# Two-block transformer on one core: GpSimd's side work tied to VectorE's search rounds, and three VectorE edits beside it

## The chip, the cores and the metric

One core of one Trainium2 chip runs the whole program. The metric is the device time of one execution in microseconds; lower is better.

## The reference, cut to what matters

Two blocks of two layers each work on 512 tokens of 1024 features in float32 (the first also on 256 context tokens). The change lies in the second block:

```python
def hybrid_layer(x, ...):
    h = rms_norm_2(x, norm1_g)
    proj = h @ w_in
    (qa, ka, va, qi, ki, wi, qb, kb, vb, rb, gl, uc) = split_cols(proj)
    ...
    o_a = dsa_attention(qa, ka, va, qi, ki, wi)   # each query keeps its 128 best keys
    log_a = log_sigmoid(gl @ w_gate_up + b_gate) / 16
    o_b = gla_chunked(qb, kb, vb, log_a)          # decays between positions: exp of differences of cumsum(log_a)
    o_c = multiscale_pool(uc, w_pool, pool_scale) # trailing means over 2, 4, 8, 16 tokens, minus the token
    x = x + concat(o_a, o_b, o_c) @ w_out
    x = x + conv_glu_ffn(rms_norm_2(x, norm2_g), ...)
```

In `dsa_attention` the scores `sum_h wi * relu(qi . ki)` are masked causally, the 128 largest of each query are kept, and the rest get minus infinity ahead of the softmax. The second block begins with the first block's final norm, so its residual x has to be multiplied once by the reciprocal root of the mean square of each token (`rs_x`).

## The kernel before, in words

Tokens run along the free dimension, features along the 128 partitions. Every product with a weight is made of three matmuls, since float32 weights and activations are each held as a high and a low part (L651 to L653, and L914 to L916 where tokens go to the partitions). Weights come as slabs of 128x1024 through two raw slots; ScalarE rounds a slab to its high part (L1421), VectorE subtracts to get the low part (L2009), and only then may TensorE use it. There are two slots for split slabs: a slab's high part is made when the slab two before it has been used, its low part has to be there one slab later.

In the input stage of each layer of the second block (`in2`) VectorE is taken up by `best_keys`: for each of three query tiles (t = 1, 2, 3, with 256, 384 and 512 keys) it adds four heads of scores (L2698, L2700), masks the diagonal square (L2705, L2706), then runs 16 search rounds of "eight largest" (L2710) and "replace them" (L2711), and turns what was replaced into the mask `far` by three operations (L2714 to L2716). Meanwhile GpSimd makes the low parts of 15 slabs (`POOL_SLABS`, L2860), which I number S0 (weights of qb) to S14 (ka 0); S2 to S8 are rb 0, rb 1, va 0 to 3 and vb 0, S9 is vb 1, S10 to S13 are qa 0 to 3. Between them it does side work in a fixed order: in layer 0 it scales the eight chunks of x (`scale_x`), in both layers the gate rows, uc, four windows of the pooling (`window`), two subtractions (L2906), and the scaling of qb, kb and rb. The slab after S14 (ka 1) is VectorE's again.

Behind the search VectorE rotates the eight tiles of qa and ka (`rope`, L2247 to L2249), one for each slab. `gate_beside` puts other work behind each rotation: `gate_sums` (cumulated gates) and the first of five `distances` behind rotation 0, distances 1 and 2 behind rotation 1, 3 behind 2, 4 behind 3. ScalarE takes the exponentials of a distance in `decays`, one rotation later than the distance was queued, and VectorE multiplies them into `qd` and `kd` in `decayed`, behind rotations 2 to 6. Each engine runs its own queue in order; semaphores tie them. The products of the second attention (L1266) wait for all ten of `decayed`'s results.

Of the kernel before, what the change touches and what calls it, by code (L numbers as in the profile page):

```python
# [19 lines left out]
DC = D // P  # L20
CTX, SEQ = 256, 512
TOK = CTX + SEQ
# [35 lines left out]
NEG = -1e30  # L58
# [252 lines left out]
def build(nc, wstream, ada_w, c_in, params, x_in, rope_tab, pos_in, cnt_in, ada_first, c_cols, out):  # L311
# [3 lines left out]
    with ctx:  # L315
# [233 lines left out]
        x_scaled = sem("x_scaled")  # L549
# [839 lines left out]
        def _(act):  # L1389
# [431 lines left out]
            def in2(l):  # L1821
# [65 lines left out]
                projections(IN2_ROPED, INDEX_ROTS, beside=lambda j: decays(j - INDEX_ROTS - 1))  # L1887
# [102 lines left out]
        def _(dve):  # L1990
# [642 lines left out]
            def in2(l):  # L2633
                dsts = {"qa": qa, "ka": ka, "qi": qi}

                def results(events, j, beside=None):
                    for kind, name, g in events:
                        if kind == "idx":
                            continue
                        res.add()  # L2640
                        if kind == "gemm":
                            split_low()
                        elif kind == "rot":
                            dve.wait_ge(acc_taken, res.now())
                            dst = ki[:, :] if name == "ki" else dsts[name[0]][:, name[1], :]
                            rope(dst, rot2[j % 2][:, :], cos2[:, :], sin2[:, :]).then_inc(rot_done, 1)
                            if beside is not None:
                                beside(j)
                            j += 1

                def gate_beside(j):

                    n = j - INDEX_ROTS
                    if n == 0:
                        gate_sums(l)
                    for lev in ((0,), (1, 2), (3,), (4,))[n] if n < 4 else ():
                        distances(lev)
                    if n == 2:
                        dve.wait_ge(qk_scaled, 2 * (l + 1))
                    if 0 <= n - 2 < len(HALVES):  # L2660
                        decayed(n - 2)

                reciprocal_roots([(DC, [(0, SEQ)], D)])
                results(IN2_INDEX[:1], 0)
                if l == 0:
                    second_roots()
                results(IN2_INDEX[1:2], 0)
                copied.add()
                dve.wait_ge(rs_ready, copied.now())
                dve.wait_ge(trig_ready, 2 * (l + 1))  # L2670
                nc.vector.tensor_tensor(cos2[:, :], cos_t[:, :], rs_in[:, :], ALU.mult).then_inc(tab_made, 1)
                nc.vector.tensor_tensor(sin2[:, :], sin_t[:, :], rs_in[:, :], ALU.mult).then_inc(tab_made, 1)
                dve.wait_ge(tab_made, 2 * (l + 1))
                results(IN2_INDEX[2:], 0)
                dve.wait_ge(acc_taken, res.now())
                tables.add(16)
                pooled[l] = (res.n + 1, tables.n, copied.n, his.n)
                best_keys()
                results(IN2_PLAIN, INDEX_ROTS)
                for slabs in (4, 2):  # L2680
                    split_low(slabs)
                    res.add(QT)
                results(IN2_ROPED, INDEX_ROTS, gate_beside)
                rots.add(IN2_ROTS)

            def best_keys():
# [3 lines left out]
                for t in range(1, QT):  # L2690
# [15 lines left out]
                    v(nc.vector.tensor_tensor(score[:, diag], score[:, diag], above, ALU.add))  # L2706
# [6 lines left out]
                    b = far[:, t, 0:nk]  # L2713
                    v(nc.vector.tensor_scalar(b, work[:, 0:nk], TAKEN, NEG, ALU.is_equal, ALU.mult))  # L2714
                    v(nc.vector.tensor_scalar(b, b, -NEG, None, ALU.add))
                    v(nc.vector.tensor_tensor(far[:, t, diag], far[:, t, diag], above, ALU.subtract))  # L2716

            def gate_sums(l):

                z = tmp[2][:, :]  # L2720
                if l == 0:
                    dve.wait_ge(x_scaled, DC)
# [127 lines left out]
        def _(pool):  # L2850
# [12 lines left out]
            def scale_x(k):  # L2863
                xk = x[:, k, CTX:TOK]
                nc.gpsimd.tensor_tensor(xk, xk, rs_x[:, :], ALU.mult).then_inc(x_scaled, 1)

# [6 lines left out]

            for l in range(LAYERS):
                slabs = iter(POOL_SLABS[l])
                result, table, copied, lows = pooled[l]
                if l == 0:
                    pool.wait_ge(rs_ready, copied)
                    pool.wait_ge(hl_ready, lows)
                    for k in range(DC - 2):  # L2880
                        scale_x(k)
                pool.wait_ge(split_done, POOL_SLABS[l].start)
                split_low(next(slabs))
                if l == 0:
                    for k in range(DC - 2, DC):
                        scale_x(k)
# [3 lines left out]
                split_low(next(slabs))  # L2890
                pool.wait_ge(rope_in, table)
# [6 lines left out]
                split_low(next(slabs))  # L2898
# [3 lines left out]
                for g, width in enumerate(POOL_WINDOWS):  # L2902
                    window(g, width)
                    split_low(next(slabs))
                for c in range(2):
# [3 lines left out]
                ins.then_inc(pool_ready, 1)  # L2909
                for n, t in enumerate((qb, kb)):  # L2910
                    split_low(next(slabs))
# [248 lines left out]
```

## Time and profile before

| | |
|---|---|
| median of 3 runs | 3659.4 us (3658.09 to 3662.3) |
| the profiled execution: own time, span | 3657.96 us, 3656.1 us |
| TensorE matmul busy | 3469.6 us, 95% |
| VectorE busy | 2121.7 us, 58% |
| ScalarE busy | 1321.5 us, 36% |
| GpSimd busy | 135.6 us, 4% |
| granted TensorE clock, mean | 0.966 |
| chain of waits, share of the span | PE 83%, DVE 11%, ACT 3% |
| input stage and what follows it, layer 0 and layer 1 | from about 2300 us and from about 2970 us |

PE is TensorE, DVE VectorE, ACT ScalarE, POOL GpSimd. TensorE is busy nearly all the time, so only what lets it wait, or lowers its clock, can move the total; GpSimd's 135.6 us lie within the two input stages alone.

### The profile page before, as it was taken

The page shows a single profiled execution, that of the slowest core. Times are in us where ns is not written, and L with a number is a line of the kernel's source. Part 1 is how long each engine was busy: PE and PEld are TensorE (multiplying, and loading weights), DVE is VectorE, ACT ScalarE, POOL GpSimd, SP SyncE. Part 2 cuts the span into 40 slices and gives each one's busy share as a digit, 9 for nine tenths or more (in the row PEclk, how much of TensorE's full clock was granted, in tenths as well). Part 3 has the DMA queues.
Part 4 walks back from the last instruction along what each step waited for, and adds up shares of the span by engine and source line. Part 5 has one row for each costly group of instructions (what it writes and reads, how often), then busy time and mean ns, then how long its engine had stood idle before and what let it go on. Part 6 is the DMA issues. An engine that isn't in the chain of part 4 may idle for free.

```text
span 3656.1 us, 45965 instructions
## 1 busy us (share of the span) xinstructions
PE 3469.6 (95%) x18168; PEld 2778.6 (76%) x18168; DVE 2121.7 (58%) x3299; ACT 1321.5 (36%) x2084; POOL 135.6 (4%) x78
## 2 busy tenths in 40 slices
PE   6999999989999989999999999987999998899998
PEld 4766778878888877677777888765888877578887
DVE  4854663355575585446447664794666449646643
ACT  3344343333213223444433333334322233532222
POOL 0000000000000000000000000530000015000000
PEclk8999999999999999999999999997999999889999
DMA  5410202112351332101222333220233332013332
GB/s 232 147 41 12 87 30 86 59 52 63 109 203 63 115 116 64 30 25 45 63 87 83 95 96 103 86 76 1 92 92 93 106 98 70 30 54 96 98 96 94
DMA packets 79221, 300.56 MB, mean 82 GB/s; under 512 B 8784, under 2 KB 8912, under 8 KB 77904
## 3 DMA queue, kind: packets, MB, share of 16 engines
q1 hardware_dynamic: 77760, 291.47, 24.9%
q10 hardware_dynamic: 1296, 6.82, 0.5%
q8 instruction: 112, 1.84, 0.2%
q14 instruction: 53, 0.43, 0.0%
HBM read 296.16 MB, written 2.10 MB: 82 GB/s over the span
## 4 chain that ended last, share of the span: by engine, by line
PE 83%; DVE 11%; ACT 3%; issue 2%; DMA 1%; SPq 0%; DVEq 0%; ACTq 0%
PE ps L651 23%; PE ps L652 22%; PE ps L653 22%; PE ps L969 2%; DVE work L2711 2%; DVE top L2710 2%; PE ps L1011 1%; PE ps L1016 1%; PE ps L1039 1%; PE ps L1025 1%; PE ps L1046 1%; DVE ps L2187 1%; DVE ada_o L2187 1%; PE ps L706 1%; DVE score L2700 1%
## 5 line engine op out<-in xcount | busy, mean ns | idle before, releaser
L2009 DVE TENSOR_TENSOR split<-raw,split 128x1024 fp32r<-128x1024 f32 x412 | 504.7, 1225 | 821.8 <-ACT split L1421 820.9
L1421 ACT ACTIVATE split<-raw 128x1024 fp32r<-128x1024 f32 x442 | 466.4, 1055 | 758.3 <-PE ps L653 670.1
L651 PE MATMUL ps<-h,split 128*128 128x512 f32 x1328 | 533.4, 402 | 13.2 <-DVE split L2009 9.6
L652 PE MATMUL ps<-h,split 128*128 128x512 f32 x1328 | 526.1, 396 | 0.0
L653 PE MATMUL ps<-h,split 128*128 128x512 f32 x1328 | 525.7, 396 | 0.0
L651 PE MATMUL ps<-h_hl,split 128*128 128x512 f32 (+1 forms) x776 | 296.4, 382 | 19.5 <-DVE h_hl L2081 14.0
L651 PEld LDWEIGHTS ps<-h,split 128*128 128x128 f32 x1328 | 251.3, 189 | 80.2 <-DVE split L2009 11.7
L652 PEld LDWEIGHTS ps<-h,split 128*128 128x128 f32 x1328 | 251.3, 189 | 60.7 <-issue 2.9
L653 PEld LDWEIGHTS ps<-h,split 128*128 128x128 f32 x1328 | 251.2, 189 | 59.4
L653 PE MATMUL ps<-h_hl,split 128*128 128x512 f32 (+1 forms) x776 | 278.8, 359 | 0.0
L652 PE MATMUL ps<-h_hl,split 128*128 128x512 f32 (+1 forms) x776 | 278.6, 359 | 0.0
L651 PE MATMUL ps<-h2w,split 128*128 128x256 f32 (+1 forms) x704 | 239.9, 341 | 5.6 <-DVE h2w L2081 3.7
L652 PE MATMUL ps<-h2w,split 128*128 128x256 f32 (+1 forms) x704 | 239.7, 340 | 0.0
L653 PE MATMUL ps<-h2w,split 128*128 128x256 f32 (+1 forms) x704 | 239.3, 340 | 0.0
L653 PE MATMUL ps<-g_hl,split 128*128 128x512 f32 x528 | 208.4, 395 | 0.0
L652 PE MATMUL ps<-g_hl,split 128*128 128x512 f32 x528 | 208.4, 395 | 0.0
L651 PE MATMUL ps<-g_hl,split 128*128 128x512 f32 x528 | 208.4, 395 | 0.0
L651 PEld LDWEIGHTS ps<-h_hl,split 128*128 128x128 f32 x776 | 151.9, 196 | 56.9 <-issue 24.6
L2328 DVE TENSOR_REDUCE stat<-ps 128x1 f32<-128x768 f32 (+1 forms) x160 | 128.5, 845 | 86.5 <-PE ps L1016 81.4
L653 PEld LDWEIGHTS ps<-h_hl,split 128*128 128x128 f32 x776 | 151.4, 195 | 21.9
L652 PEld LDWEIGHTS ps<-h_hl,split 128*128 128x128 f32 x776 | 152.3, 196 | 18.2 <-issue 1.4
L1601 ACT ACTIVATE prob<-ps,stat 128x768 f32<-128x768 f32 (+1 forms) x160 | 128.9, 813 | 102.6 <-DVE stat L2328 102.6
(410 smaller groups left out, 6297.6 us busy)
## 6 DMA issues: line engine op xcount, KB each, us to landing
raw<-wstream SPq DMA_DIRECT2D x442, 512.0 KB, 3.5
ada_t<-ada_w SPq DMA_DIRECT2D x80, 512.0 KB, 4.6
first_w<-ada_first SPq DMA_DIRECT2D x4, 2048.0 KB, 24.8
x<-x_in SPq DMA_DIRECT2D x1, 3072.0 KB, 12.7
x<-x_in ACTq DMA_DIRECT2D x1, 3072.0 KB, 11.0
ada_c<-c_in SPq DMA_DIRECT2D x2, 1024.0 KB, 4.7
out<-x SPq DMA_DIRECT2D x8, 256.0 KB, 2.2
par<-params SPq DMA_DIRECT2D x1, 1345.0 KB, 5.8
```

Of the source, the lines that this page charges most:

```text
L651: nc.tensor.matmul(o, wh, a[0], start=first, stop=False)
L652: nc.tensor.matmul(o, wh, a[1], start=False, stop=False)
L653: return nc.tensor.matmul(o, wl, a[0], start=False, stop=last)
L706: mm = nc.tensor.matmul(ps[h * n:(h + 1) * n, ACC_BANKS + t // QT, (t % QT) * P:(t % QT + 1) * P], rstd[:, j * heads + h:j * heads + h + 1 ...
L969: mm = nc.tensor.transpose(ps[:, 4 + t // 4, (t % 4) * P:(t % 4 + 1) * P], p[:, t * P:(t + 1) * P], col("ident", 0, P))
L1421: nc.scalar.activation(split[:, n % SPLIT_SLOTS, 0, :], raw[:, n % RAW_SLOTS, :], copy).then_inc(hi_split, 1)
L1601: nc.scalar.activation(prob[l][i % 2][:, a, 0:nk], banks(2 * a, nk), ACT.Exp, bias=st[:, a:a + 1], scale=-1.0, accum_out=st[:, 2 + a:3 + a ...
L2009: nc.vector.tensor_tensor(split[:, n % SPLIT_SLOTS, 1, :], raw[:, n % RAW_SLOTS, :], split[:, n % SPLIT_SLOTS, 0, :].bitcast(F32), ALU.sub ...
L2187: ins = nc.vector.tensor_tensor_reduce(out=ada_out if group == 1 else banks(6, D), in0=w, in1=ada_c[group][:, j, :], scale=1.0, scalar=0.0 ...
L2328: nc.vector.tensor_reduce(st[:, a:a + 1], banks(2 * a, steps[i][2]), AX.X, ALU.min).then_inc(s_max, 1)
L2710: v(nc.vector.max(top8[:, :], src[:, 0:nk]))
L2711: v(nc.vector.match_replace(work[:, 0:nk], top8[:, :], src[:, 0:nk], TAKEN))
```

## The change

GpSimd no longer scales x; VectorE does so behind the two rotation tables. GpSimd's side work is cut in three packets, and each waits by the semaphore `search_on` for the start of a search (16 rounds) of its layer. The mask `far` takes one operation in place of three. `gate_sums` and all five `distances` move ahead of rotation 0, and `decayed` moves from behind rotations 2 to 6 to behind rotations 1 to 5; ScalarE's `decays` move one rotation earlier too.

```diff
@@ ScalarE, in2
-                projections(IN2_ROPED, INDEX_ROTS, beside=lambda j: decays(j - INDEX_ROTS - 1))
+                projections(IN2_ROPED, INDEX_ROTS, beside=lambda j: decays(j - INDEX_ROTS))
@@ VectorE, gate_beside
-                    if n == 0:
-                        gate_sums(l)
-                    for lev in ((0,), (1, 2), (3,), (4,))[n] if n < 4 else ():
-                        distances(lev)
-                    if n == 2:
+                    if n == 1:
                         dve.wait_ge(qk_scaled, 2 * (l + 1))
-                    if 0 <= n - 2 < len(HALVES):
-                        decayed(n - 2)
+                    if 0 <= n - 1 < len(HALVES):
+                        decayed(n - 1)
@@ VectorE, in2
                 dve.wait_ge(tab_made, 2 * (l + 1))
+                if l == 0:
+                    for k in range(DC):
+                        xk = x[:, k, CTX:TOK]
+                        nc.vector.tensor_tensor(xk, xk, rs_x[:, :], ALU.mult)
                 results(IN2_INDEX[2:], 0)
...
                     split_low(slabs)
                     res.add(QT)
+                gate_sums(l)
+                for lev in range(len(HALVES)):
+                    distances(lev)
                 results(IN2_ROPED, INDEX_ROTS, gate_beside)
@@ VectorE, best_keys
-                    v(nc.vector.tensor_tensor(score[:, diag], score[:, diag], above, ALU.add))
+                    nc.vector.tensor_tensor(score[:, diag], score[:, diag], above, ALU.add).then_inc(search_on, 1)
+                    searches.add()
+                    dve.wait_ge(search_on, searches.now())
...
-                    b = far[:, t, 0:nk]
-                    v(nc.vector.tensor_scalar(b, work[:, 0:nk], TAKEN, NEG, ALU.is_equal, ALU.mult))
-                    v(nc.vector.tensor_scalar(b, b, -NEG, None, ALU.add))
-                    v(nc.vector.tensor_tensor(far[:, t, diag], far[:, t, diag], above, ALU.subtract))
+                    v(nc.vector.tensor_scalar(far[:, t, 0:nk], work[:, 0:nk], TAKEN, -NEG, ALU.not_equal, ALU.mult))
@@ GpSimd
+            def beside_search(l, t):
+                pool.wait_ge(search_on, (QT - 1) * l + t)
...
-                if l == 0:
-                    pool.wait_ge(rs_ready, copied)
-                    pool.wait_ge(hl_ready, lows)
-                    for k in range(DC - 2):
-                        scale_x(k)
                 pool.wait_ge(split_done, POOL_SLABS[l].start)
                 split_low(next(slabs))
-                if l == 0:
-                    for k in range(DC - 2, DC):
-                        scale_x(k)
...
                 split_low(next(slabs))
+                beside_search(l, 1)
...
                 pool.wait_ge(gl_scaled, l + 1)
-                split_low(next(slabs))
                 v(nc.gpsimd.tensor_tensor(uc[:, :, PAD:], uc[:, :, PAD:], both, ALU.mult))
                 split_low(next(slabs))
-                for g, width in enumerate(POOL_WINDOWS):
-                    window(g, width)
+                window(0, POOL_WINDOWS[0])
+                split_low(next(slabs))
+                split_low(next(slabs))
+                beside_search(l, 2)
+                for g in range(1, len(POOL_WINDOWS)):
+                    window(g, POOL_WINDOWS[g])
                     split_low(next(slabs))
+                split_low(next(slabs))
+                beside_search(l, 3)
...
                 ins.then_inc(pool_ready, 1)
+                split_low(next(slabs))
                 for n, t in enumerate((qb, kb)):
-                    split_low(next(slabs))
```

How the queues stand, at the two places of which the prediction speaks. First GpSimd in layer 0, from the pooling's last window (L2870, L2872 before, L2868, L2870 now) to the scaling of rb. Before:

```order
L2870 TENSOR_TENSOR win_286<-win_285 128x2x512
L2872 TENSOR_TENSOR tmp_281<-win_286,cnt 64x512
L2860 TENSOR_TENSOR split<-raw,split 128x1024
L2906 TENSOR_TENSOR tmp_280<-tmp_280,uc 128x512
L2906 TENSOR_TENSOR tmp_281<-tmp_281,uc 128x512
L2860 TENSOR_TENSOR split<-raw,split 128x1024
L2913 TENSOR_TENSOR qb<-qb,rs_in 128x512
L2860 TENSOR_TENSOR split<-raw,split 128x1024
L2913 TENSOR_TENSOR kb<-kb,rs_in 128x512
L2860 TENSOR_TENSOR split<-raw,split 128x1024
L2916 TENSOR_TENSOR rb<-rb,rs_in 128x1024
```

and now:

```order
L2868 TENSOR_TENSOR win_286<-win_285 128x2x512
L2870 TENSOR_TENSOR tmp_281<-win_286,cnt 64x512
L2862 TENSOR_TENSOR split<-raw,split 128x1024 x2
L2906 TENSOR_TENSOR tmp_280<-tmp_280,uc 128x512
L2906 TENSOR_TENSOR tmp_281<-tmp_281,uc 128x512
L2862 TENSOR_TENSOR split<-raw,split 128x1024
L2913 TENSOR_TENSOR qb<-qb,rs_in 128x512
L2913 TENSOR_TENSOR kb<-kb,rs_in 128x512
L2862 TENSOR_TENSOR split<-raw,split 128x1024
L2916 TENSOR_TENSOR rb<-rb,rs_in 128x1024
```

Two splits, S7 and S8, now stand between the last window and the subtractions, and it is ahead of the first subtraction that GpSimd waits for the third search; S9 and all later splits are queued behind that wait.

Second VectorE in layer 0 behind the third search, from rotation 0 (of `qa`, L2247 to L2249) to distances 1. Before:

```order
L2716 TENSOR_TENSOR far<-far,par 128x128
L2247 TENSOR_TENSOR rot_289<-rot_289,sin_257 128x512
L2248 TENSOR_TENSOR qa<-qa,cos_256 128x512
L2249 TENSOR_TENSOR qa<-qa,rot_289 128x512
L2723 MEMSET ones_291 128x512
L2725 SCALAR_TENSOR_TENSOR tmp_282<-tmp_282,tmp_283 128x512
L2726 SCALAR_TENSOR_TENSOR gcum<-ones_291,tmp_282 128x512
L2736 TENSOR_TENSOR tmp_282<-gcum 128x512
L2739 TENSOR_SCALAR qd<-tmp_282 128x512
L2740 TENSOR_SCALAR kd<-tmp_282 128x512
L2247 TENSOR_TENSOR rot_288<-rot_288,sin_257 128x512
```

and now, from the last distance (the one row of `far` and four more distances stand ahead of it) to the first split of a slab (L2009, ka 1):

```order
L2742 TENSOR_SCALAR kd<-tmp_282 128x512
L2247 TENSOR_TENSOR rot_289<-rot_289,sin_257 128x512
L2248 TENSOR_TENSOR qa<-qa,cos_256 128x512
L2249 TENSOR_TENSOR qa<-qa,rot_289 128x512
L2247 TENSOR_TENSOR rot_288<-rot_288,sin_257 128x512
L2248 TENSOR_TENSOR qa<-qa,cos_256 128x512
L2249 TENSOR_TENSOR qa<-qa,rot_288 128x512
L2749 SCALAR_TENSOR_TENSOR qd<-qb,qd 128x512
L2751 TENSOR_TENSOR kd<-kb,kd 128x512
L2009 TENSOR_TENSOR split<-raw,split 128x1024
```

Ahead of that split stood two rotations and three distances; now two rotations, five distances and the first `decayed` stand there.

## Rows read from the trace of the kernel before

**Rows 1.** Waits of PE, 2290 to 2480 us (layer 0): total, times, longest

```profile
PE ps L651 <- DVE split L2009: 3.7, 1, 3.7
PE ps L669 <- ACT qa L1408: 3.0, 1, 3.0
PE ps L1266 <- DVE kd L2749: 2.7, 1, 2.7
...
PE ps L1246 <- DVE ki L2249: 0.6, 1, 0.6
```

**Rows 2.** Waits of PE, 2960 to 3160 us (layer 1)

```profile
PE ps L669 <- ACT qa L1408: 3.1, 1, 3.1
```

**Rows 3.** Timeline of PE, layer 0: start, busy us, work, [idle before]

```profile
2433.52 1.12 PE L669 MATMUL ps<-qa,par 128*128 128x512 f32 x2 [3.03 <-ACT qa L1408]
2438.29 0.80 PE L651 MATMUL ps<-h,split 128*128 128x512 f32 x1 [3.65 <-DVE split L2009]
...
2441.45 0.63 PE L652 MATMUL ps<-h,split 128*128 128x512 f32 x1
...
2464.95 5.32 PE L1266 MATMUL ps<-qd,kd 32*128 32x256 f32 x80 [2.71 <-DVE kd L2749]
```

**Rows 4.** Windows: stretch, us, busy us of PE, PEld, DVE, ACT, POOL, PEclk, DMA

```profile
2440.00:2442.00 2.00, 2.00 (x6) 1.52 (x6) 1.97 (x5) 0.00 (x0) 0.00 (x0) 0.50 0.60 238
```

**Rows 5.** Timeline of ACT, layer 0

```profile
2431.83 0.63 ACT L1896 ACTIVATE qd<-qd 128x512 f32<-128x512 f32 x1 [10.85 <-DVE qd L2739]
...
2462.28 0.69 ACT L1408 ACTIVATE mix<-ps,par 128x512 f32<-128x512 f32 x1 [0.17 <-PE ps L1256]
```

**Rows 6.** Timeline of POOL, layer 0

```profile
2356.50 2.41 POOL L2860 TENSOR_TENSOR split<-raw,split 128x1024 fp32r<-128x1024 f32 x1 [2.07 <-ACT split L1421]
...
2379.86 2.67 POOL L2906 TENSOR_TENSOR tmp<-tmp,uc 128x512 f32<-128x512 f32 x2
...
2394.72 2.40 POOL L2860 TENSOR_TENSOR split<-raw,split 128x1024 fp32r<-128x1024 f32 x1 [2.51 <-ACT split L1421]
...
2412.84 2.40 POOL L2860 TENSOR_TENSOR split<-raw,split 128x1024 fp32r<-128x1024 f32 x1 [3.20 <-ACT split L1421]
2419.27 2.41 POOL L2860 TENSOR_TENSOR split<-raw,split 128x1024 fp32r<-128x1024 f32 x1 [4.03 <-ACT split L1421]
```

**Rows 7.** Timeline of DVE, layer 0, up to the third search

```profile
2320.98 1.54 DVE L2009 TENSOR_TENSOR split<-raw,split 128x1024 fp32r<-128x1024 f32 x1 [5.67 <-ACT split L1421]
...
2336.59 2.59 DVE L2700 SCALAR_TENSOR_TENSOR score<-relu,wi,score 128x256 f32<-128x256 f32 x3
...
2355.62 0.29 DVE L2714 TENSOR_SCALAR far<-work 128x256 f32<-128x256 f32 x1
...
2356.60 2.53 DVE L2698 TENSOR_SCALAR score<-relu,wi 128x384 f32<-128x384 f32 x1
2359.16 6.34 DVE L2700 SCALAR_TENSOR_TENSOR score<-relu,wi,score 128x384 f32<-128x384 f32 x3
...
2368.81 0.56 DVE L2710 MAX8 top<-score 128x8 f32<-128x384 f32 x1
...
2388.83 2.22 DVE L2714 TENSOR_SCALAR far<-work 128x384 f32<-128x384 f32 x1
...
2400.41 0.69 DVE L2710 MAX8 top<-score 128x8 f32<-128x512 f32 x1
```

**Rows 8.** Timeline of DVE, layer 0, from the end of the third search

```profile
2424.68 0.43 DVE L2714 TENSOR_SCALAR far<-work 128x512 f32<-128x512 f32 x1
...
2428.14 0.48 DVE L2723 MEMSET ones<- 128x512 f32 x1
...
2432.05 0.68 DVE L2247 TENSOR_TENSOR rot<-rot,sin 128x512 f32<-128x512 f32 x1
...
2437.02 1.22 DVE L2009 TENSOR_TENSOR split<-raw,split 128x1024 fp32r<-128x1024 f32 x1
```

**Rows 9.** Groups of DVE, 2312 to 2470 us: count, busy us, mean ns

```profile
L2710 DVE MAX8 top<-work 128x8 f32<-128x512 f32 x15 | 10.4, 695 | 0.5
```

More of the change, by code:

```diff
@@ L548, in build @@
         rb_scaled = sem("rb_scaled")
-        x_scaled = sem("x_scaled")
+        search_on = sem("search_on")
         pooled = {}
@@ L2676, in in2 @@
                 tables.add(16)
-                pooled[l] = (res.n + 1, tables.n, copied.n, his.n)
+                pooled[l] = (res.n + 1, tables.n, copied.n)
                 best_keys()
@@ L2712, in best_keys @@
                         src = work
-                    b = far[:, t, 0:nk]
-                    v(nc.vector.tensor_scalar(b, work[:, 0:nk], TAKEN, NEG, ALU.is_equal, ALU.mult))
-                    v(nc.vector.tensor_scalar(b, b, -NEG, None, ALU.add))
-                    v(nc.vector.tensor_tensor(far[:, t, diag], far[:, t, diag], above, ALU.subtract))
+                    v(nc.vector.tensor_scalar(far[:, t, 0:nk], work[:, 0:nk], TAKEN, -NEG, ALU.not_equal, ALU.mult))
+            searches = Count()
             def gate_sums(l):
                 z = tmp[2][:, :]
-                if l == 0:
-                    dve.wait_ge(x_scaled, DC)
                 v(nc.vector.memset(ones2[:, :], 1.0))
@@ L2861, in split_low @@
                                         split[:, n % SPLIT_SLOTS, 0, :].bitcast(F32), ALU.subtract).then_inc(split_done, 1)
-            def scale_x(k):
-                xk = x[:, k, CTX:TOK]
-                nc.gpsimd.tensor_tensor(xk, xk, rs_x[:, :], ALU.mult).then_inc(x_scaled, 1)
             def window(g, width):
@@ L2872, in window @@
                 v(nc.gpsimd.tensor_tensor(tmp[c][r, :], to[r, c, PAD:], cnt[r, c, :], ALU.mult))
+            def beside_search(l, t):
+                pool.wait_ge(search_on, (QT - 1) * l + t)
             for l in range(LAYERS):
                 slabs = iter(POOL_SLABS[l])
-                result, table, copied, lows = pooled[l]
-                if l == 0:
-                    pool.wait_ge(rs_ready, copied)
-                    pool.wait_ge(hl_ready, lows)
-                    for k in range(DC - 2):
-                        scale_x(k)
+                result, table, copied = pooled[l]
                 pool.wait_ge(split_done, POOL_SLABS[l].start)
                 split_low(next(slabs))
-                if l == 0:
-                    for k in range(DC - 2, DC):
-                        scale_x(k)
                 v(nc.gpsimd.memset(uc[:, :, 0:PAD], 0.0))
```

## The prediction, made before the changed kernel ran

> **What bounds the kernel now.** I read the page's busy times first: TensorE is at work for 95% of the span, so the change can only pay where TensorE waits or runs at a lower clock. The waits of PE in the two input stages name those places. In layer 0 TensorE waits 3.0 us for the taking of qa by ScalarE, 3.7 us for a low part by VectorE, 2.7 us for `kd` and 0.6 us for the rotated `ki` [rows 1]; layer 1 repeats the first three, with 3.1 for the first [rows 2]. The timeline of PE puts the first two side by side, at 2430 and 2434 us, and shows what follows: matmuls of 0.63 us instead of the 0.40 of the page's mean, from 2438.29 until past 2441.45 [rows 3]. The granted clock of the window from 2440 to 2442 us is 0.50 [rows 4], the lower of the two levels, 1.2 instead of 2.4 GHz: 3.6 us at half speed, of which some 1.7 are lost.
>
> Both waits are one lateness of VectorE. ScalarE stood 10.85 us in front of the first exponential of `decays` because `qd` was not there, with qa's result behind it in its queue [rows 5], and the low part of ka 1 came at 2437.02 [rows 8]. VectorE had left the third search only at 2424.68 [rows 8] and had all of the rotations and distances still to do. So the question is what makes the searches end so late. The timelines of DVE and POOL, laid beside each other, answer: a 384-wide `TENSOR_SCALAR`, some 0.4 us of work, took 2.53 us from 2356.60 [rows 7], just while GpSimd made S4 from 2356.50 to 2358.91 [rows 6]; the three score operations behind it took 6.34 us instead of about 1.8; and of the mask's three operations the first took 2.22 us at 384 columns, where it had taken 0.29 at 256 without GpSimd beside it [rows 7]. The two engines exclude each other for a whole instruction. The search rounds do not take part: a 512-wide "eight largest" took 0.69 us at 2400.41 [rows 7] and 695 ns in the mean of the 15 that followed [rows 9], with splits on GpSimd at 2412.84 and 2419.27 that kept their own 2.4 us too [rows 6]. The Trainium skill, SBUF — State Buffer, "Who interferes with whom", says the same as a rule on inputs: a VectorE instruction with two SBUF inputs contends with a GpSimd one that reads SBUF, one with a single input outside the 2-port modes does not. By this rule the cumulated sum of the gates (two inputs) would be stopped as well; no row here shows it. If it were free, about 1 us less of the collisions below would be left in each layer.
>
> **The sum, part by part.** *Side work beside the searches.* In layer 0 GpSimd's gate rows lie in the three 256-wide scores, which took 2.59 us [rows 7] instead of 1.3; they move behind the search's start, so search 1 ends 1.3 us earlier, at 2354.3 instead of 2355.6. The mask is now one operation, 0.3. Four 384-wide score operations and two on the diagonal are 2.8 us when nothing disturbs them (two inputs of 512 columns take 0.68 [rows 8], so I take about 0.56 for 384 and 0.3 for 128). One split, S4, still falls there, since ScalarE releases it at about 2356: 2.4 us. Search 2 then begins at 2359.9 instead of 2368.8, lasts the same 20.0 us (2368.81 to 2388.83) [rows 7] and ends at 2379.9. Mask 0.4, scores 3.3, S8 (released at about 2382) 2.4: search 3 begins at 2386.0 instead of 2400.4 [rows 7], lasts 24.3 (2400.41 to 2424.68) [rows 7, 8] and is done with its mask at 2410.7, against 2425.9: 15.2 us earlier.
>
> *What now stands ahead of the first split.* Gate sums with the first distance took 3.91 us (2428.14 to 2432.05), a rotation and two distances 4.97 (2432.05 to 2437.02) [rows 8]. A rotation is three operations of 0.68, 2.05 together, so a distance is 1.46. The changed queue needs 3.9 + 4 x 1.46 = 9.8 for gates and distances, 4.1 for two rotations, 1.3 for `decayed` (two of 0.68), 1.2 for the split: 16.4 us. And since this now begins at 2410.7, GpSimd's S13 and S14 (at 2412.84 and 2419.27 before) [rows 6] fall into the distances, where they fell into the search: each stops VectorE for its 2.4 us, 4.8 together (not under 2.4, as one falls there surely, and not over 7.2, if S12 came too). The low part of ka 1 is ready at 2431.9 instead of 2438.2: 6.3 us gained, of the 15.2. TensorE would need it at about 2431.1, 0.6 less for the wait on `ki` that is gone: so about 1.4 us of the wait stays, and with it I keep the slow matmuls. ScalarE's earlier `decays` cost nothing: the first distance is ready at about 2417, when TensorE is just done with qa 2.
>
> *Ten results of `decayed` one rotation earlier.* They are done a slab earlier (6.4 us), so the products of the second attention wait for ScalarE's `mix`, ready at 2462.97, instead of starting at 2464.95 [rows 3, 5]: 1.9 us, ends 0 and 2.7.
>
> *x by VectorE.* Eight operations of 0.68 us at most, 5.4 together, lie in a hole of 5.67 us ahead of the split at 2320.98 [rows 7]; cover enough. If that cover were gone the split would come up to 5 us later, which TensorE would see only in part, since the slab is used a slab later. GpSimd loses the eight operations, and with them the stops that made `ki` late: that is the 0.6 us, counted above.
>
> *Layer 1* has no x and no wait for `ki`, and its first scores run into GpSimd's second split instead of beside it; I take 1 us less, 5.3. Its other terms are the same.
>
> Sum: 6.3 + 5.3 + 2 x 1.9 = 15.4 us; 3658.0 - 15.4 = 3642.6, against the profiled execution's own 3657.96, which lies 1.4 under the median of the runs. I say **3643 us**.
>
> **Rivals.** *No wait left.* If S13 and S14 cost VectorE 1.5 us less than I took, or the scores gain more, both waits and the slow matmuls vanish: 2 x (3.0 + 3.7 + 1.7 + 1.9) + 0.6 = 21 us, 3637. For it speaks that only some 1.4 us are missing; against it, that each collision so far cost the full 2.4.
>
> *GpSimd tied to a late search.* S9 and all behind it wait for search 3. vb 1 must be split when TensorE is done with vb 0, about 2393.0 [rows 6]: S10 followed the use of vb 0 and was released at 2394.7, a ScalarE split of 1.05 after it, and 0.6 comes off. Subtractions 2.67 and split 2.41 go ahead, so search 3 has to begin by 2387.9; I have 2386.0. Past that point TensorE stands for each microsecond. Did the searches begin as late as before, at 2400.4, the split of ka 1 would come at 2424.7 + 0.5 + 16.4 + 4.8 = 2446.4, 8.2 later than before; less 1.9, twice, 12.6 us slower: **3671**. It decides from a start of 2394.2 on, where the gain is nil; under that it eats it. Against it: the scores' stops are plain in the rows, and only S4 and S8 stay.
>
> *ScalarE stuck in front of `decays` 0.* It now waits one rotation earlier, with qa 2 and the high part for S14 behind it. If the first distance comes 3 us later than I have it, S14 is late and TensorE waits for it: some 3 us less in each layer, 3649.
>
> *The lateness is not the collisions'.* Then search 3 hardly moves, and only `decayed` and the mask are left: about 4 us, within no change, but GpSimd's wait then bites too, as above.
>
> **Numbers.** The forecast 0.56, no wait left 0.24, ScalarE stuck 0.11, GpSimd tied to a late search 0.05, hardly a gain 0.04. Range 3636 to 3650: it takes in the first three, with the ends of their terms. A measurement of this kernel can tell about 0.2% from no change, some 7 us: faster 0.90, same 0.05, slower 0.05.
>
> **What would show it.** In the changed profile: scores of tile 2 and 3 with one stop each; search 3 beginning near 2386; the split of ka 1 near 2432; distances stopped twice by GpSimd; a wait of 1 to 2 us of TensorE there in each layer, followed by slow matmuls; no wait on `kd`, one of under 1 us on `mix` in its place; no wait on `ki`; x's eight operations between 2314 and 2320. I am wrong if TensorE waits for a split by GpSimd anywhere, or if search 3 starts after 2388.

## The result, and the profile after

| | before | changed |
|---|---|---|
| median of 6 runs | 3660.85 us (3654.43 to 3665.53) | 3634.03 us (3627.89 to 3637.91) |
| ratio, 95% interval | | 0.9927 [0.9915, 0.994] |
| profiled execution: own time, span | 3657.96, 3656.1 us | 3633.83, 3632.0 us |
| matmul busy, mean granted clock | 3469.6 us, 0.966 | 3459.5 us, 0.973 |

The change is faster, by 24.1 us in the profiled executions and 26.8 in the medians. The prediction, 3643 us with a range from 3636 to 3650, had the sign and too small a gain: the result lies 2 us below the range.

The waits of TensorE in the input stage of layer 0 come first, as engine, output and line, releaser, total, times and longest. They answer to [rows 1].

```profile
PE ps L651 <- DVE split L2009: 2.1, 1, 2.1
...
PE ps L1266 <- ACT mix L1408: 0.8, 1, 0.8
```

The waits for qa and `ki` are gone, the one for the low part is down from 3.7 to 2.1 us, and `mix` has taken the place of `kd`, for 0.8 us instead of 2.7. The timeline of PE in the changed kernel shows what stands behind those waits, first layer 0 and, after the third line of dots, layer 1 [rows 3].

```profile
2431.14 0.50 PE L651 MATMUL ps<-h,split 128*128 128x512 f32 x1 [2.05 <-DVE split L2009]
...
2434.35 0.63 PE L653 MATMUL ps<-h,split 128*128 128x512 f32 x1
...
2455.73 3.46 PE L1266 MATMUL ps<-qd,kd 32*128 32x256 f32 x80 [0.78 <-ACT mix L1408]
2460.92 4.98 PE L1266 MATMUL ps<-qd,kd 32*128 32x256 f32 x80 [1.73 <-ACT att_off L1922]
2467.58 1.65 PE L1316 MATMUL ps<-ka,qa 64*128 64x128 f32 x8 [1.68 <-ACT att_off L1922]
...
3090.82 0.50 PE L651 MATMUL ps<-h,split 128*128 128x512 f32 x1 [1.31 <-DVE split L2009]
...
3113.84 3.46 PE L1266 MATMUL ps<-qd,kd 32*128 32x256 f32 x80 [0.78 <-ACT mix L1408]
3119.02 4.37 PE L1266 MATMUL ps<-qd,kd 32*128 32x256 f32 x80 [1.72 <-ACT att_off L1922]
3125.07 1.65 PE L1316 MATMUL ps<-ka,qa 64*128 64x128 f32 x8 [1.68 <-ACT att_off L1922]
```

The rows of the kernel before that stand against the last three lines of each layer were not shown yet:

```profile
2471.90 6.26 PE L1266 MATMUL ps<-qd,kd 32*128 32x256 f32 x80 [1.63 <-ACT att_off L1922]
2479.84 1.65 PE L1316 MATMUL ps<-ka,qa 64*128 64x128 f32 x8 [1.68 <-ACT att_off L1922]
...
3134.12 5.47 PE L1266 MATMUL ps<-qd,kd 32*128 32x256 f32 x80 [2.71 <-DVE kd L2749]
3141.21 6.26 PE L1266 MATMUL ps<-qd,kd 32*128 32x256 f32 x80 [1.63 <-ACT att_off L1922]
3149.15 1.65 PE L1316 MATMUL ps<-ka,qa 64*128 64x128 f32 x8 [1.68 <-ACT att_off L1922]
```

Here is the part of the gain that the prediction did not have. The 80 products with `kd` took 5.32 and 5.47 us before and take 3.46 in both layers now; the 80 behind them took 6.26 and take 4.98 and 4.37. The windows of the two traces say why. Their columns are the stretch, us, busy us of PE, PEld, DVE, ACT and POOL, then the granted clock, DMA share and GB/s. Before:

```profile
2467.00:2470.00 3.00, 3.00 (x60) 2.66 (x61) 1.06 (x2) 0.00 (x0) 0.00 (x0) 0.50 0.00 0
2475.00:2478.00 3.00, 3.00 (x64) 2.66 (x60) 0.00 (x0) 0.00 (x0) 0.00 (x0) 0.50 0.03 5
```

And the same work in the changed kernel:

```profile
2455.00:2459.00 4.00, 3.27 (x79) 2.98 (x80) 3.90 (x7) 1.83 (x3) 0.00 (x0) 1.00 0.45 131
2461.00:2464.00 3.00, 3.00 (x32) 2.98 (x32) 0.00 (x0) 0.00 (x0) 0.00 (x0) 0.72 0.00 0
```

After a wait of 2.7 us the products ran at a granted clock of 0.50 (1.2 GHz) for most of their time. After a wait of 0.8 us the first 80 ran at 1.00 (2.4 GHz), and the second 80 fell to the low level only on their way.

VectorE's timeline in layer 0 answers to [rows 7, 8], and is what the prediction's working was about.

```profile
2314.17 4.91 DVE L2673 TENSOR_TENSOR x<-x,rs_x 128x512 f32<-128x512 f32 x8
...
2336.52 1.53 DVE L2703 SCALAR_TENSOR_TENSOR score<-relu,wi,score 128x256 f32<-128x256 f32 x3
...
2354.48 0.29 DVE L2718 TENSOR_SCALAR far<-work 128x256 f32<-128x256 f32 x1
...
2355.27 3.96 DVE L2703 SCALAR_TENSOR_TENSOR score<-relu,wi,score 128x384 f32<-128x384 f32 x3
...
2380.33 2.52 DVE L2701 TENSOR_SCALAR score<-relu,wi 128x512 f32<-128x512 f32 x1
...
2385.89 0.69 DVE L2715 MAX8 top<-score 128x8 f32<-128x512 f32 x1
...
2410.18 0.43 DVE L2718 TENSOR_SCALAR far<-work 128x512 f32<-128x512 f32 x1
...
2411.30 2.24 DVE L2727 SCALAR_TENSOR_TENSOR tmp<-tmp,tmp 128x512 f32<-128x512 f32 x1
2413.58 1.23 DVE L2728 TENSOR_TENSOR_SCAN gcum<-ones,tmp 128x512 f32<-128x512 f32 x1
...
2418.96 2.63 DVE L2742 TENSOR_SCALAR kd<-tmp 128x512 f32<-128x512 f32 x1
...
2429.86 1.22 DVE L2009 TENSOR_TENSOR split<-raw,split 128x1024 fp32r<-128x1024 f32 x1
```

GpSimd's timeline gives the partners of the stretched instructions [rows 6].

```profile
2355.68 2.48 POOL L2862 TENSOR_TENSOR split<-raw,split 128x1024 fp32r<-128x1024 f32 x1 [4.96 <-ACT split L1421]
2359.95 1.89 POOL L2868 TENSOR_TENSOR win<-win 128x1024 f32<-128x1024 f32 x1 [1.80 <-DVE score L2709]
...
2380.06 2.50 POOL L2862 TENSOR_TENSOR split<-raw,split 128x1024 fp32r<-128x1024 f32 x1 [2.43 <-ACT split L1421]
2385.94 2.66 POOL L2906 TENSOR_TENSOR tmp<-tmp,uc 128x512 f32<-128x512 f32 x2 [3.38 <-DVE score L2709]
...
2410.59 2.40 POOL L2862 TENSOR_TENSOR split<-raw,split 128x1024 fp32r<-128x1024 f32 x1 [3.17 <-ACT split L1421]
2418.69 2.61 POOL L2862 TENSOR_TENSOR split<-raw,split 128x1024 fp32r<-128x1024 f32 x1 [5.69 <-ACT split L1421]
```

The scores of tiles 2 and 3 have one stop each, by the splits at 2355.68 and 2380.06: an instruction is stopped when it has to stand until the other engine's is over, and its own row gets longer by that. The windows (2359.95) and the subtractions (2385.94) begin right behind the scores' end. The third search starts when its scores are done, at 2385.9, and its mask is done at 2410.6. The splits at 2410.59 and 2418.69 stop the gates (2.24 us) and one distance (2.63 us).

### The profile page after: what moved, and what is told of

The parts are those of the page before. It is cut to its first block, busy times and chain, and to the rows that moved or that the text cites. A ratio compares the mean times of both kernels' runs of the same rounds, so it can differ in the third digit from the quotient of the medians.

```text
span 3632.0 us, 45947 instructions
## 1 busy us (share of the span) xinstructions
PE 3459.5 (95%) x18168; PEld 2771.1 (76%) x18168; DVE 2102.3 (58%) x3295; ACT 1321.1 (36%) x2084; POOL 121.8 (3%) x70
## 4 chain that ended last, share of the span: by engine, by line
PE 82%; DVE 11%; ACT 3%; DMA 2%; issue 2%; SPq 0%; DVEq 0%; ACTq 0%
PE ps L651 22%; PE ps L653 22%; PE ps L652 22%; PE ps L969 2%; DVE work L2716 2%; DVE top L2715 2%; PE ps L1011 2%; PE ps L1016 1%; PE ps L1039 1%; PE ps L1025 1%; PE ps L1046 1%; DVE ps L2187 1%; DVE ada_o L2187 1%; PE ps L706 1%; ACT split L1421 1%
## 5 line engine op out<-in xcount | busy, mean ns | idle before, releaser
L2009 DVE TENSOR_TENSOR split<-raw,split 128x1024 fp32r<-128x1024 f32 x412 | 504.4, 1224 | 821.6 <-ACT split L1421 820.7
L2862 POOL TENSOR_TENSOR split<-raw,split 128x1024 fp32r<-128x1024 f32 x30 | 72.7, 2424 | 2943.8 <-ACT split L1421 2943.0
```

The lines of the kernel that those rows point to most:

```text
L2009: nc.vector.tensor_tensor(split[:, n % SPLIT_SLOTS, 1, :], raw[:, n % RAW_SLOTS, :], split[:, n % SPLIT_SLOTS, 0, :].bitcast(F32), ALU.sub ...
L2862: nc.gpsimd.tensor_tensor(split[:, n % SPLIT_SLOTS, 1, :], raw[:, n % RAW_SLOTS, :], split[:, n % SPLIT_SLOTS, 0, :].bitcast(F32), ALU.sub ...
```

## The experiments

All eight were timed beside the kernel before: late_kd, spread, old_order and no_pool_wait on one chip, after_again, order_only, mask3 and x_pool on another. Times before the stage differ from run to run with the same code: VectorE's first score of layer 0 began at 2334.2 and at 2327.6 us in the two profiles of the changed kernel. So beside the medians I read one stretch of each profile, from the start of that first score to the start of the attention (the row of PE, L1316; in x_pool that line is L1317). It holds the searches, the split, both waits and the products. "Products" are the first and second 80.

| kernel | ratio | stage, layer 0 | layer 1 | products, layer 0 | layer 1 |
|---|---|---|---|---|---|
| before | 1 | 145.6 | 144.9 | 5.32, 6.26 | 5.47, 6.26 |
| changed | 0.9927 [0.9915, 0.994] | 133.4 | 132.0 | 3.46, 4.98 | 3.46, 4.37 |
| after_again | 0.9937 [0.9921, 0.9953] | 133.4 | 132.2 | 3.85, 6.26 | 3.46, 4.47 |
| late_kd | 0.9966 [0.9953, 0.998] | 138.1 | 137.1 | 4.99, 6.26 | 4.88, 6.26 |
| spread | 0.992 [0.9907, 0.9932] | 130.8 | 132.3 | 3.46, 6.26 | 3.46, 6.26 |
| old_order | 0.9966 [0.9954, 0.9979] | 135.4 | 137.0 | 6.26, 6.26 | 6.26, 6.26 |
| no_pool_wait | 1.0001 [0.9992, 1.001] | 145.9 | 145.9 | 4.09, 6.26 | 4.12, 6.26 |
| order_only | 1.0006 [0.9995, 1.0016] | 145.2 | 146.0 | 3.46, 6.26 | 3.46, 6.26 |
| mask3 | 0.9958 [0.9942, 0.9974] | 138.4 | 136.1 | 3.46, 6.26 | 3.46, 4.81 |
| x_pool | 0.995 [0.9935, 0.9964] | 135.2 | 132.2 | 3.46, 6.27 | 3.46, 4.59 |

For before and changed the stage gives 12.2 + 13.0 = 25.2 us; 1.1 of it is lost again behind the stage of layer 0, and 24.1 is the difference of the profiles. The loss lies in the attention: TensorE's first matmul on `mix_hl`, the one behind a wait of 3.64 us in both, starts 79.7 us after the attention's start before (2559.57 us) and 80.7 in the changed kernel (2548.32), with a granted clock of 0.79 and 0.75 in the some 20 us ahead of it.

**The last `decayed` late again (late_kd).** Theory A says that the wait for `kd` costs twice, once as a wait and once through the clock of the products behind it; the rival that it costs its 1.9 us only.

```diff
-                    if 0 <= n - 1 < len(HALVES):
+                    if 0 <= n - 1 < len(HALVES) - 1:
                         decayed(n - 1)
+                    if n == len(HALVES) + 1:
+                        decayed(len(HALVES) - 1)
```

> The changed kernel with one edit: the last of the five decayed steps goes back behind rotation 6, as in the kernel before. Theory A (the clock is the missing part): the wait of TensorE on kd (2.7 us) comes back in both layers, the 80 products behind it take 5.3 us again instead of 3.5 and the next 80 about 6.3 instead of 4.4 to 5.0, so the start of the attention comes 5 to 6 us later in each layer and the run 9 to 12 us later than the changed kernel's. Theory B (the products got faster for another reason, for instance by where they happened to fall): only the 1.9 us of the wait come back in each layer, the products keep 3.5 us, and the run is some 4 us later.

3645.62 us (3633.25 to 3648.59), where the kernel before on that chip took 3654.61. The timeline of PE:

```profile
2431.74 0.50 PE L651 MATMUL ps<-h,split 128*128 128x512 f32 x1 [2.05 <-DVE split L2009]
...
2458.23 4.99 PE L1266 MATMUL ps<-qd,kd 32*128 32x256 f32 x80 [2.71 <-DVE kd L2753]
2464.85 6.26 PE L1266 MATMUL ps<-qd,kd 32*128 32x256 f32 x80 [1.63 <-ACT att_off L1922]
```

Its window, with the columns as above:

```profile
2460.00:2463.00 3.00, 3.00 (x64) 2.66 (x61) 1.34 (x3) 0.00 (x0) 0.00 (x0) 0.50 0.00 0
```

The split wait is the same 2.05 us, so nothing ahead of the products has changed. The wait grew by 1.93 us in each layer, and the stage by 4.7 and 5.2. The products alone account for the rest: 1.53 + 1.28 in layer 0, 1.42 + 1.89 in layer 1. Theory A holds: a wait of 2.7 us at this place costs more again in clock than in waiting.

The stage says this more safely than the products. The second profile of the changed kernel (after_again, below) has the same short wait and stages as long, but in layer 0 products of 3.85 and 6.26 us; against it late_kd also loses 4.7 us in layer 0, of which 1.9 are the wait, 1.1 the products and 1.5 slow matmuls behind the split, which that profile lacked. Added up over windows of 1 us, waits included, the granted clock stood at the low level for 24.1 and 24.4 us of the two stages before, 8.7 and 7.4 in the changed kernel, 10.7 and 7.6 in after_again, and 16.6 and 16.4 in late_kd. And the loss does not end with the stage: late_kd's profile is 14.8 us longer than the changed kernel's, of which 9.8 lie in the stages, 2.7 between them, 1.7 behind the second and 0.6 ahead of the first. The medians, 9.0 us under the kernel before for late_kd and 26.8 and 25.5 for the changed kernel, lie still farther apart than the 9 to 12 us expected; late_kd's times are spread over 15 us, and the two were not timed on one chip.

**GpSimd's waits taken away (no_pool_wait).**

```diff
             def beside_search(l, t):
-                pool.wait_ge(search_on, (QT - 1) * l + t)
+                pass
```

> The changed kernel with GpSimd's three waits on the searches taken out and its new order of work kept. Theory: the waits are what keeps side work out of the scores; without them the subtractions (2.67 us), windows and scalings run ahead as before and stop VectorE's scores and masks again; search 3 begins 5 to 12 us later than 2385.9, the wait on VectorE's first split grows by about the same and the run comes out 10 to 20 us over the changed kernel. Rival: the new order alone does it, since x is gone from GpSimd and splits stand in pairs; then search 3 begins within 2 us of 2386 and the run is within 3 us of the changed kernel's.

The whole gain is gone. VectorE's timeline of this kernel:

```profile
2331.85 4.59 DVE L2703 SCALAR_TENSOR_TENSOR score<-relu,wi,score 128x256 f32<-128x256 f32 x3
...
2356.86 2.42 DVE L2701 TENSOR_SCALAR score<-relu,wi 128x384 f32<-128x384 f32 x1
2359.31 4.35 DVE L2703 SCALAR_TENSOR_TENSOR score<-relu,wi,score 128x384 f32<-128x384 f32 x3
...
2387.08 5.25 DVE L2703 SCALAR_TENSOR_TENSOR score<-relu,wi,score 128x512 f32<-128x512 f32 x3
```

All three tiles' scores are stopped again, and the third search starts at 2395.1 although this run's first score was 4.7 us earlier than the changed kernel's: 13.9 us later, counted from there, where 5 to 12 were expected. The loss, 26 us in the two stages, is above the expected 10 to 20 too. PE then waits elsewhere:

```profile
2425.34 2.08 PE L669 MATMUL ps<-qa,par 128*128 128x512 f32 x2 [6.74 <-ACT qa L1408]
2428.93 0.80 PE L651 MATMUL ps<-h,split 128*128 128x512 f32 x1 [1.52 <-POOL split L2862]
...
2438.71 0.50 PE L651 MATMUL ps<-h,split 128*128 128x512 f32 x1 [1.06 <-DVE split L2009]
```

This is the rival "ScalarE stuck in front of `decays` 0": qa's result waits 6.7 us behind an exponential whose distance comes late, and the high part for GpSimd's last split behind it. It bites only when the searches end late.

**The order of the change alone, on the kernel before (order_only).** The gates and distances stand right behind the search and `decays` and `decayed` one rotation earlier, all else as before.

```diff
-                projections(IN2_ROPED, INDEX_ROTS, beside=lambda j: decays(j - INDEX_ROTS - 1))
+                projections(IN2_ROPED, INDEX_ROTS, beside=lambda j: decays(j - INDEX_ROTS))
...
+                gate_sums(l)
+                for lev in range(len(HALVES)):
+                    distances(lev)
                 results(IN2_ROPED, INDEX_ROTS, gate_beside)
```

> The kernel before with one part of the change: gates and all distances ahead of rotation 0, and decays and decayed steps one rotation earlier. Theory: with the searches still ending at 2424.7 the first split of VectorE comes 3 distances and a decayed step later less one rotation's worth of nothing, 2424.7 + 1.25 + 16.4 = 2442.3 instead of 2438.2, so the waits of TensorE ahead of it grow by 4 us in each layer; the wait on kd goes and with it 4.5 to 5.5 us in each layer: within 4 us of the kernel before. Rival: the order is what brings the gain, and the run lies 8 us or more under the kernel before.

3654.75 us beside 3655.38: nothing. The product times are those of the good case, 3.46 and 6.26, since the wait for `kd` is gone; what that gives, the timeline of PE takes back at the same place as above:

```profile
2427.88 2.08 PE L669 MATMUL ps<-qa,par 128*128 128x512 f32 x2 [7.40 <-ACT qa L1408]
2431.47 0.79 PE L651 MATMUL ps<-h,split 128*128 128x512 f32 x1 [1.51 <-POOL split L2859]
```

The size was as expected, the place of the wait was not: it grew at qa, from 3.0 to 7.4 us, not at the split.

**The old order on the changed kernel (old_order).** The diff of order_only the other way round.

> The changed kernel with the order behind the search as it was before (distances, decays and decayed steps), so that only GpSimd's packets, x on VectorE and the one-operation mask are left of the change. Theory A: VectorE's first split stands behind 12.3 us of work from the end of the search at 2410.7, plus two stops by GpSimd, so it is ready by 2428 and TensorE doesn't wait for it (gain of 7 to 9 us a layer kept); the wait of 2.7 us on kd and the slow products come back, 5 to 6 us a layer, less the 2 to 3.5 us that the wait on the split costs the changed kernel: 4 to 8 us over the changed kernel, about 3640. Theory B (no clock part in the products): within 2 us of the changed kernel.

3641.59 us (3637.07 to 3645.69), where the kernel before on that chip took 3654.61. No wait is left ahead of the split, as the earlier searches give enough room; but `kd` is late by 2.71 us in both layers, and all four sets of products run at the low clock, 6.26 us. The stage is 2.0 and 5.0 us longer than with the new order. So the order is worth some 7 us in the stages once the searches are early, and nothing while they are late. (The medians give more, 13.0 us under the kernel before here against 25.5 and 26.8 for the changed kernel, but on different chips.)

**The mask in three operations again (mask3).**

```diff
-                    v(nc.vector.tensor_scalar(far[:, t, 0:nk], work[:, 0:nk], TAKEN, -NEG, ALU.not_equal, ALU.mult))
+                    b = far[:, t, 0:nk]
+                    v(nc.vector.tensor_scalar(b, work[:, 0:nk], TAKEN, NEG, ALU.is_equal, ALU.mult))
+                    v(nc.vector.tensor_scalar(b, b, -NEG, None, ALU.add))
+                    v(nc.vector.tensor_tensor(far[:, t, diag], far[:, t, diag], above, ALU.subtract))
```

> The changed kernel with the mask in three operations again. Theory: three masks take 0.7 us more each and push the scores behind them against GpSimd's S4 and S8 no differently, so search 3 begins 1.4 us later (2387.3) and VectorE's split comes 2.2 us later; TensorE's wait on it grows to about 4 us in layer 0 and 3.5 in layer 1: 4 to 6 us over the changed kernel. Rival: the later search also holds GpSimd's S9, which TensorE then waits for, and the run is 8 us or more over it.

3639.21 us, 9.3 over the changed kernel on the same chip; the stage says 5.0 + 4.1 = 9.1, where 4 to 6 were expected. VectorE's timeline first:

```profile
2377.83 2.10 DVE L2719 TENSOR_SCALAR far<-work 128x384 f32<-128x384 f32 x1
...
2408.97 2.62 DVE L2720 TENSOR_SCALAR far<-far 128x512 f32<-128x512 f32 x1
```

Two of its operations ran into splits and took 2.10 and 2.62 us in place of 0.36 and 0.43: a stopped operation waits for what is left of the other engine's instruction on top of its own time. But these two stops came in place of two of the changed kernel's, not on top of them: the score operation behind the first took 0.49 us instead of 2.52, and the gates' operation behind the second 0.69 instead of 2.24. Counted from the first score, TensorE gets its low part 2.5 us later in layer 0 and 2.1 in layer 1, about the 2.2 expected. The rest is the clock of TensorE's work: from that part to the products it needs 1.2 and 1.5 us more, and for the second 80 products 1.3 and 0.4. TensorE's timeline in layer 0:

```profile
2389.32 0.39 PE L914 MATMUL ps<-split,h 128*128 128x256 f32 x1 [0.93 <-POOL split L2865]
...
2430.87 0.79 PE L651 MATMUL ps<-h,split 128*128 128x512 f32 x1 [3.06 <-DVE split L2009]
```

The second wait is 3.06 us in both layers, under the 4 and 3.5 expected. The first is the rival "GpSimd tied to a late search": the third search began 52.8 us after the first score instead of 51.7, and TensorE stood 0.93 us for S9, which is queued behind it. It cost nothing by itself here, since TensorE waits for VectorE farther on. But the changed kernel has no room left there either: its S9 was done at 2390.95 (2388.56 + 2.39, GpSimd's timeline), and TensorE's first matmul with it started at 2391.00.

**x scaled by GpSimd again (x_pool).**

```diff
-                if l == 0:
-                    for k in range(DC):
-                        xk = x[:, k, CTX:TOK]
-                        nc.vector.tensor_tensor(xk, xk, rs_x[:, :], ALU.mult)
...
+            def scale_x(k):
+                xk = x[:, k, CTX:TOK]
+                nc.gpsimd.tensor_tensor(xk, xk, rs_x[:, :], ALU.mult).then_inc(x_scaled, 1)
...
```

The lines left out call it for six chunks ahead of S0 and two behind it, and let VectorE wait for x ahead of the gates.

> The changed kernel with x scaled by GpSimd again, six chunks ahead of S0 and two behind it. Theory: ki is rotated 2 us later in layer 0, TensorE waits 0.6 us for it as before, VectorE's searches hardly move since the scores wait for ScalarE's relu: within 1 us of the changed kernel. Rival: the two scalings behind S0 push S1 and the scores; then search 1 begins over 1 us later and the wait on VectorE's split grows by as much, 2 to 4 us over it in all.

3636.54 us beside 3629.91 for the changed kernel, more than the 1 us expected; but the intervals overlap, and in the profiles the stage differs by 1.8 us in layer 0 and by nothing in layer 1, where x is not scaled. The wait of 0.6 us for `ki`, which lies ahead of the stage, is back. So scaling on VectorE is worth between 0.6 us and a few; the rest of the distance between the medians was not traced to anything.

**Distances and decays spread over the rotations (spread).** Gate sums and two distances ahead of the first rotation, the rest one or two behind each, so that the splits of VectorE come earlier; `kd` stays in time.

```diff
-                    if 0 <= n - 1 < len(HALVES):
-                        decayed(n - 1)
+                    for kind, lev in {0: (("d", 2),), 1: (("d", 3),), 2: (("d", 4), ("x", 0)), 3: (("x", 1), ("x", 2)), 4: (("x", 3),), 5: (("x", 4),)}.get(n, ()):
+                        (distances if kind == "d" else decayed)(lev)
...
-                for lev in range(len(HALVES)):
+                for lev in range(2):
                     distances(lev)
```

> The changed kernel with the distances spread again: gates and distances 0 and 1 ahead of rotation 0, distance 2 behind it, distance 3 behind rotation 1, distance 4 behind rotation 2, and all decayed steps done by rotation 5 as in the change. Ahead of VectorE's first split stand one distance and one decayed step less, 2.8 us. Theory A: the wait on that split, 2.05 us in layer 0 and 1.31 in layer 1, is the lateness of VectorE alone, so it vanishes in both layers, the slow matmuls behind it in layer 0 go too (1.7 us), and the run is 4 to 5 us under the changed kernel's, near 3629. Rival: GpSimd's splits S13 and S14 or ScalarE's queue set that time; the wait stays over 1 us and the run within 1 us of the changed kernel's.

3626.56 us (3622.23 to 3628.17), 28.1 under the kernel before on that chip, the lowest median of all. The timeline of PE:

```profile
2450.61 6.26 PE L1266 MATMUL ps<-qd,kd 32*128 32x256 f32 x80 [1.73 <-ACT att_off L1922]
2458.55 1.65 PE L1316 MATMUL ps<-ka,qa 64*128 64x128 f32 x8 [1.68 <-ACT att_off L1922]
```

The split wait is gone in both layers, and the first products begin 3.9 us earlier in layer 0, counted from the first score (117.7 us after it instead of 121.6), and 1.6 us earlier in layer 1. But the second 80 products, which in the changed kernel's first profile had fallen to the low clock on their way, now run at it from their start to their end: 6.26 in place of 4.98 and 4.37, so that 1.3 and 1.9 us go back. What is left of the stage is 2.6 us in layer 0 and nothing in layer 1. For layer 0 this is one reading of two: after_again has 6.26 there as well with the split wait in place, so the slow products need not come from the wait's being gone. For layer 1 both profiles of the changed kernel have less (4.37 and 4.47). Its interval overlaps with both of the changed kernel's, which was timed in other sets of runs: a gain over it is possible and small, and is not shown.

**The changed kernel again (after_again).** Unedited, as the measure for the second chip.

> The changed kernel itself, unedited, as the measure for the kernels beside it. Theory: 20 to 30 us under the kernel before, with the waits of its first profile (2.05 and 1.31 us on VectorE's split, 0.78 on mix). Rival: its first profile was lucky in where the clock fell, and 15 us are nearer to what it gains.

3629.91 us (3625.49 to 3636.89) beside 3655.38. The stage repeats to 0.2 us, though the clock fell at other places. In layer 0 no matmul behind the split wait (2.03 us) was slow, and the products took more:

```profile
2447.57 3.85 PE L1266 MATMUL ps<-qd,kd 32*128 32x256 f32 x80 [0.78 <-ACT mix L1408]
2453.05 6.26 PE L1266 MATMUL ps<-qd,kd 32*128 32x256 f32 x80 [1.63 <-ACT att_off L1922]
```

## Why the prediction was right and wrong

*Collisions and searches: right.* The third search was put at 2386.0 and started at 2385.9; the mask was to be done at 2410.7 and was at 2410.6; one split stops each of the tiles 2 and 3, and the search rounds take 695 ns as before [rows 9]. no_pool_wait shows that this is where the gain comes from: with only the three waits taken out, the stage is 145.9 us in both layers, as before. That answers the rival by which the lateness was not the collisions'.

*The split of ka 1: right in kind, a little small.* It was put at 2431.9 and was ready at 2431.1. Two collisions fell into the gates and distances as foreseen, but cost 2.24 - 0.69 and 2.63 - 0.42, together 3.8 us in layer 0 and not the 4.8 I took from two whole splits: an instruction that meets a split already under way loses only what is left of it. In layer 0 the gain up to the next result was 7.3 us (6.3 predicted); the slow matmuls stayed, as kept, from 2431.8 to 2434.8 us. In layer 1 the split itself gained 5.65 (5.3 predicted), and here the slow matmuls, which I had kept, did not come behind a wait of 1.31 us: 1.6 us more. This term of the sum was 2.9 us too small over both layers. (In layer 1 the first of the two stops fell on the cumulated sum of the gates, see the last section.)

*`decayed` one rotation earlier: the step that failed.* "1.9 us, ends 0 and 2.7" is right for the wait: 1.9 us measured in both layers (2.71 less 0.78). What was missing is the clock of the work behind it, a cost that the sum put at nothing. I had charged slow matmuls behind the split wait [rows 3, 4] and had the row with 80 products in 5.32 us [rows 3] on the page, and did not ask whether the same thing happened there. With the wait cut to 0.8 us the stretch from the products' start to the attention got shorter by 3.0 us in layer 0 and 3.8 in layer 1; 1.1 was given back in the attention of layer 0. late_kd puts the wait back and loses 2.8 and 3.3 us of it in products alone, 4.7 and 5.2 us of the stage in all. The sum, corrected: 15.4 + 2.9 + 6.8 - 1.1 = 24.0, against 24.1.

*x by VectorE: right.* 4.91 us for 5.4, in the hole it was given; the wait for `ki` is gone.

*The rivals.* "No wait left", at 3637, is the nearest in time, but not what happened: waits of 2.05 and 1.31 us are left, and what the sum lacked came mostly from the clock. "ScalarE stuck" did not occur in the changed kernel, and does in no_pool_wait and order_only, with 6.7 and 7.4 us: right as a mechanism. Its price of 3 us was not tried: there the first distance came some 12 us later than in the changed kernel, not 3. "GpSimd tied to a late search" did not come in the changed kernel, but by less than I thought. I had TensorE stand for GpSimd from a search start of 2387.9 on, 2.0 us behind the one measured; mask3 shows a wait of 0.93 us for S9 with a start only 1.1 us later, and in the changed kernel S9 was done at 2390.95 and used at 2391.00. TensorE wanted vb 1 at 2391.0, not at "about 2393.0": the point lies at the measured start itself.

*What stays open.* What decides where the clock falls. Behind a wait of 0.78 us the first 80 products took 3.46 to 4.12 us and behind one of 2.71 us 4.88 to 6.26 over all profiles, so the wait tells the two groups apart but not the time within them. For the second 80 not even that: the same wait of 1.73 us stood ahead of 4.98 us of them in the changed kernel and 6.26 in spread. In the changed kernel's layer 0 the slow matmuls at 2363 to 2367 us, behind a wait of 1.16 us, are gone too (1.6 us), though they stay in layer 1; no edit here aimed at them. TensorE came to the split that much earlier and waited longer for it, 2.05 us in layer 0 against 1.31 in layer 1. And the changed kernel and spread were not timed beside each other on one chip.

## What to carry to other kernels

When a wait of TensorE is taken away, price the matmuls behind it too: look up their duration at either level of the granted clock, and charge the difference, here 2.8 to 3.8 us behind a wait that itself was worth 1.9. And where two engines stop each other, place the side work beside instructions that take no part in it (here the search rounds), before moving anything else: the new order alone gave nothing, and some 7 us once the searches were early.

For a difference of a few us, compare a stretch between two events of the profile rather than whole times; it repeated to 0.2 us in two profiles of one kernel while its whole times were 11 us apart.

## What the runs showed that I had not expected

The cumulated sum of the gates is stopped by GpSimd as well. In the changed kernel it took 1.23 us in layer 0 and this in layer 1, where VectorE's timeline and then GpSimd's read:

```profile
3071.10 3.39 DVE L2728 TENSOR_TENSOR_SCAN gcum<-ones,tmp 128x512 f32<-128x512 f32 x1
```

```profile
3071.01 2.40 POOL L2862 TENSOR_TENSOR split<-raw,split 128x1024 fp32r<-128x1024 f32 x1 [3.20 <-ACT split L1421]
```

It is an instruction with two inputs, and the prediction had said that no row showed such a stop. The Trainium skill, SBUF — State Buffer, "Who interferes with whom", has it so by its rule on inputs, and this row agrees with 3.39 us against 1.23. The profiles of late_kd, spread, x_pool and after_again repeat it in layer 1 with 3.38 to 3.41 us. The stops are not limited to two inputs: the `TENSOR_SCALAR`s of a distance (2.63 us in place of 0.42) and of mask3's mask (2.62 in place of 0.43) have one.

The second surprise is that a removed wait can be given back by the clock. In spread 1.6 us less ahead of the products in layer 1 left nothing, with no wait put in their place: only 80 products that took 6.26 us at a granted clock of 0.50, where they had taken 4.37 and 4.47 in the changed kernel's two profiles. It is one profile of spread, and it shows that this can happen, not that it must.
